# A feed-forward stage's weight sums, from VectorE to accumulating DMAs of GpSimd, with another order of products

## The reference

```
h = h + mixed @ w_out
u = relu(rms_norm(h, norm_ffn) @ w_up)      # 1024 -> 4096
y = h + (u * u) @ w_down                    # 4096 -> 1024
```

## Time and profile before

| | |
|---|---|
| median of 3 runs | 1353.36 us (1352.21 to 1353.92) |
| profiled execution, device time | 1355.98 us |
| its span, first to last instruction | 1353.9 us |
| mean granted TensorE clock | 0.997 |

### The profile page before, as it was taken

The page is one execution under the profiler, slowest core; times in us unless marked ns, Lnnn a source line. Parts: engine busy times, 40 slices in busy tenths (PEclk is TensorE's granted clock), DMA queues, the critical chain, the costliest instruction groups (busy, mean ns, idle before and its releaser), DMA issues.

```text
span 1353.9 us, 31255 instructions
## 1 busy us (share of the span) xinstructions
PE 1330.7 (98%) x10947; PEld 1267.4 (94%) x10947; DVE 880.7 (65%) x1805; ACT 658.6 (49%) x1617; POOL 277.5 (20%) x469
## 2 busy tenths in 40 slices
PE   7999999999999999999999999999999999999998
PEld 7877888999999999999989998899999999999998
DVE  5775665446657566475564666555569978868688
ACT  5653333366656556566553555532234444344442
POOL 0510000255545555455510000000230000000000
PEclk9999999999999999999999999999999999999999
DMA  6033221466555555665544645334341332423412
GB/s 248 20 100 108 80 84 57 146 178 186 160 150 167 173 160 160 174 183 153 164 154 163 208 147 192 121 103 125 106 157 50 102 133 63 141 63 95 140 46 97
DMA packets 110645, 177.92 MB, mean 131 GB/s; under 512 B 13217, under 2 KB 84706, under 8 KB 108770
## 3 DMA queue, kind: packets, MB, share of 16 engines
q1 hardware_dynamic: 110498, 176.05, 42.2%
HBM read 163.98 MB, written 11.89 MB: 130 GB/s over the span
## 4 chain that ended last, share of the span: by engine, by line
PE 86%; DVE 3%; issue 1%; ACT 1%; POOL 0%; ACTq 0%; DVEq 0%; POOLq 0%
PE ps L1382 27%; PE ps L2617 14%; PE ps L2640 10%; PE ps L1844 10%; PE ps L1669 8%; PE ps L659 5%; PE ps L1408 2%; PE ps L725 1%; PE ps L745 1%; PE ps L1398 1%; PE ps L1895 1%; PE ps L1884 1%; PE ps L735 1%; PE ps L1898 1%; PE ps L1390 0%
## 5 line engine op out<-in xcount | busy, mean ns | idle before, releaser
L1382 PE MATMUL ps<-wq_hi,ct_hi 128*128 128x260 f32 x1024 | 301.4, 294 | 1.4 <-POOL ct_lo L1064 1.4
L1382 PE MATMUL ps<-wq_hi,ct_lo 128*128 128x260 f32 x1024 | 289.5, 283 | 0.0
L1382 PE MATMUL ps<-wq_lo,ct_hi 128*128 128x260 f32 x1024 | 289.3, 283 | 0.0
L1229 DVE TENSOR_REDUCE k_sums<-k_squares 128x8 f32<-128x512 f32 (+1 forms) x256 | 175.2, 684 | 174.3 <-ACT k_squares L1127 171.9
L1064 POOL TENSOR_TENSOR ct_lo<-ct_raw,ct_hi 128x256 fp32r<-128x256 f32 x256 | 188.8, 738 | 359.6 <-ACT ct_hi L1120 197.1
L1127 ACT ACTIVATE k_squares<-ps 128x512 f32<-128x512 f32 x256 | 153.2, 598 | 169.5 <-PE ps L1382 165.3
L1382 PEld LDWEIGHTS ps<-wq_hi,ct_hi 128*128 128x128 f32 x1024 | 193.1, 189 | 4.9 <-issue 3.8
L1382 PEld LDWEIGHTS ps<-wq_lo,ct_hi 128*128 128x128 f32 x1024 | 193.2, 189 | 0.0
L1382 PEld LDWEIGHTS ps<-wq_hi,ct_lo 128*128 128x128 f32 x1024 | 192.6, 188 | 0.0
L1844 PE MATMUL ps<-x_hi,ring_hi 128*128 128x260 f32 x384 | 113.2, 295 | 1.4 <-DVE gates L2073 1.4
L1844 PE MATMUL ps<-x_lo,ring_hi 128*128 128x260 f32 x384 | 108.5, 283 | 0.0
(11 more groups left out here) (369 smaller groups left out, 3452.7 us busy)
## 6 DMA issues: line engine op xcount, KB each, us to landing
ct_raw<-in_ct SPq DMA_DIRECT2D x256, 144.0 KB, 2.3
c_values<-in_c SPq DMA_DIRECT2D x256, 128.0 KB, 2.4
ring_raw<-in_wmain SPq DMA_DIRECT2D x40, 512.0 KB, 4.2
ring_raw<-in_up SPq DMA_DIRECT2D x16, 512.0 KB, 3.5
ff_raw<-in_up SPq DMA_DIRECT2D x16, 512.0 KB, 4.6
ring_raw<-in_down SPq DMA_DIRECT2D x16, 512.0 KB, 3.5
ff_raw<-in_down SPq DMA_DIRECT2D x16, 512.0 KB, 3.5
z_scratch<-z_staged SPq DMA_DIRECT2D x16, 268.0 KB, 4.5
```

The costliest lines, as they stand in the source:

```text
L1229: dve.tensor_reduce(to, k2[:, j].rearrange("p b h d -> p (b h) d"), AX.X, ALU.add).then_inc(red_done, 1)
L1382: mm = nc.tensor.matmul(k_ps[j % 2][:, f, 0:WQN], ch[:, j, r * P:(r + 1) * P], of_sequence(w, b)[:, r, f, :], start=(r == 0 and x == 0), s ...
```

## The change

The four sums of a step are no longer made by VectorE. ScalarE writes -a0, -a1 and -a0 into the buffers of P6, P3 and P7 (`negate`). SP loads b0 from memory a second time, straight into P5's buffer. GpSimd then issues four DMAs that add to what is there: b1 onto P5's buffer (from memory), P5's sum onto P6's, P6's sum onto P3's, and b0 onto P7's (from memory). Of tile b only the second half is still loaded into the raw buffer. P3's and P7's sums now have the opposite sign, and so have B22 and T3. The weights of w_down are laid out on the host so that a half is contiguous.

The order of a step is P1, P5, P6, P3, P7, P2, P4, step after step with no interleaving. ScalarE's upper parts run two events behind and VectorE's lower parts three. The blocks of u are made one by one in the order in which the products use them, and the last of those of the final two up tiles are made in the down stage, after the additions of P1 and P5 of step 0.

```diff
     def gpsimd(self, pool):
         self.after.gpsimd(pool)
+        self.last.gpsimd(pool)
...
-P1, P2, P6, P5, P7, P3, P4 = range(UNITS)
+P1, P5, P6, P3, P7, P2, P4 = range(UNITS)
-ORDER = [(0, P1), (1, P1), (0, P2), (1, P2)] + [(d, x) for d in range(2) for x in (P6, P5, P7, P3, P4)] + [(d, x) for d in (2, 3) for x in range(UNITS)]
+ORDER = [(d, x) for d in range(STEPS_DOWN) for x in range(UNITS)]
+PLACE = {P2: (0, 0), P3: (0, 1), P4: (1, 0), P7: (1, 1)}
+SCALED = [(d, x) for d, x in ORDER if x in PLACE]
...
-ADDS_AHEAD = 4
+HI_BEHIND, LO_BEHIND = 2, 3
...
-BEHIND = _behind()
+HI_AFTER, LO_AFTER = _behind(HI_BEHIND), _behind(LO_BEHIND)
+NEGATED = {2: [(0, P6), (0, P3), (0, P7)], 6: [(1, P6)], 8: [(1, P3)], 9: [(1, P7)]}
+NEGATED.update({AT[d - 2, P4] + n: [(d, x)] for d in (2, 3) for n, x in enumerate((P6, P3, P7))})
...
-        a, b = (self.raw[n][:].rearrange("p (k two) n -> p two k n", two=2) for n in (2 * d % 4, 2 * d % 4 + 1))
+        a, b = (self.raw[n][:].rearrange("p (two k) n -> p two k n", two=2) for n in (2 * d % 4, 2 * d % 4 + 1))
...
+    def down(self, c, t, half):
+
+        return self.m.d_down[c // 2][c % 2][t][:, 4 * half:4 * half + 4, :]
+
+    def sum_ready(self, engine, n, x):
+
+        if x == P7:
+            engine.wait_ge(self.diff_sum, 16 * n + 16)
+        else:
+            engine.wait_ge(self.chain_sums, 48 * n + {P5: 16, P6: 32, P3: 48}[x])
+
+    def sum_split(self, engine, n, x):
+
+        c, d = divmod(n, STEPS_DOWN)
+        self.split(engine, PER_CHUNK * c + AT[d, x])
...
-                    d = (n0 - UP_TILES) // 2
-                    self.split(sp, PER_CHUNK * c0 + AT[d, P4 if n0 % 2 else P2])
-                    sp.wait_ge(self.summed, self.sums_at(c0, d, P7 if n0 % 2 else P3))
-            src = m.d_up[UP_TILES * c + n] if n < UP_TILES else m.d_down[c // 2][c % 2][n - UP_TILES]
-            sp.dma_start(self.raw[r % 4][:], src).then_inc(self.loaded[r % 4], 16)
+                    d0 = (n0 - UP_TILES) // 2
+                    self.split(sp, PER_CHUNK * c0 + AT[d0, P4 if n0 % 2 else P2])
+                    if n0 % 2 == 0:
+                        sp.wait_ge(self.negated, 3 * (STEPS_DOWN * c0 + d0) + 3)
+            raw = self.raw[r % 4]
+            if n < UP_TILES:
+                sp.dma_start(raw[:], m.d_up[UP_TILES * c + n]).then_inc(self.loaded[r % 4], 16)
+            elif n % 2 == 0:
+                sp.dma_start(raw[:], m.d_down[c // 2][c % 2][n - UP_TILES]).then_inc(self.loaded[r % 4], 16)
+            else:
+                sp.dma_start(raw[:, 4:8, :], self.down(c, n - UP_TILES, 1)).then_inc(self.loaded[r % 4], 16)
+                g = STEPS_DOWN * c + (n - UP_TILES) // 2
+                if g:
+                    self.sum_split(sp, g - 1, P5)
+                    self.sum_ready(sp, g - 1, P6)
+                sp.dma_start(self.sums[P5][:], self.down(c, n - UP_TILES, 0)).then_inc(self.plain_in, 16)
...
         elif x in self.sums:
-            act.wait_ge(self.summed, self.sums_at(c, d, x))
+            self.sum_ready(act, STEPS_DOWN * c + d, x)
...
+    def negate(self, act, c, d, x):
+
+        g, r = STEPS_DOWN * c + d, 16 * c + UP_TILES + 2 * d
+        act.wait_ge(self.loaded[r % 4], self.loads(r))
+        if g:
+            self.sum_split(act, g - 1, x)
+        if g and x == P6:
+            self.sum_ready(act, g - 1, P3)
+        half = 4 * (x == P3)
+        self.nc.scalar.activation(self.sums[x][:], self.raw[r % 4][:, half:half + 4, :], ACT.Copy, scale=-1.0).then_inc(self.negated, 1)
...
                 self.made(act, e)
-                wait(act, self.u_lo, 4 * (4 * c + i))
+                wait(act, self.u_lo, 7 * pair)
                 nc.scalar.activation(self.rl[s][:], ps[s][:, :, 0:HF], ACT.Relu).then_inc(self.relu, 1)
                 act.wait_ge(self.relu, UP_TILES * c + j + 1)
                 if s == 0:
-                    nc.scalar.activation(self.uh[:, B11, i, :], self.rl[0][:, 0, :], ACT.Square).then_inc(self.u_hi, 1)
+                    nc.scalar.activation(uh[:, B11, i, :], self.rl[0][:, 0, :], ACT.Square).then_inc(self.u_hi, 1)
+                    act.wait_ge(self.u_step, 6 * pair + 2)
+                    nc.scalar.activation(uh[:, T1, i, :], t[:, 0, :], ACT.Copy).then_inc(self.u_hi, 1)
                 else:
-                    nc.scalar.activation(self.uh[:, B21:B22 + 1, i, :], self.rl[1][:], ACT.Square).then_inc(self.u_hi, 1)
-                    for n in range(2):
-                        act.wait_ge(self.u_step, 6 * (4 * c + i) + 4 + 2 * n)
-                        nc.scalar.activation(self.uh[:, T1 + 2 * n:T3 + 2 * n, i, :], self.t[:, 2 * n:2 * n + 2, :], ACT.Copy).then_inc(self.u_hi, 1)
-            for n in REFILLED[e]:
-                self.split_hi(act, n)
+                    nc.scalar.activation(uh[:, B21, i, :], self.rl[1][:, 0, :], ACT.Square).then_inc(self.u_hi, 1)
+                    act.wait_ge(self.u_step, 6 * pair + 4)
+                    nc.scalar.activation(uh[:, T2, i, :], t[:, 1, :], ACT.Copy).then_inc(self.u_hi, 1)
+                    nc.scalar.activation(uh[:, B22, i, :], self.sq[1][:, 1, :], ACT.Copy, scale=-1.0).then_inc(self.u_hi, 1)
+                    act.wait_ge(self.u_step, 6 * pair + 5)
+                    nc.scalar.activation(uh[:, T3, i, :], t[:, 2, :], ACT.Copy).then_inc(self.u_hi, 1)
+                    act.wait_ge(self.u_step, 6 * pair + 6)
+                    nc.scalar.activation(uh[:, T4, i, :], t[:, 3, :], ACT.Copy).then_inc(self.u_hi, 1)
+            for done in HI_AFTER[e]:
+                for n in REFILLED[done]:
+                    self.split_hi(act, n)
+            for d1, x1 in NEGATED.get(e % PER_CHUNK, ()):
+                self.negate(act, c, d1, x1)
...
+        def low(kind, i, of, at):
+
+            dve.wait_ge(self.u_hi, at)
+            tt(self.ul[:, kind, i, :], of, self.uh[:, kind, i, :].bitcast(F32), ALU.subtract).then_inc(self.u_lo, 1)
...
+            dve.wait_ge(self.relu, UP_TILES * c + 2 * i + 1)
+            wait(dve, self.u_step, 6 * pair)
+            wait(dve, self.u_lo, 7 * pair)
+            tt(self.sq[0][:], self.rl[0][:], self.rl[0][:], ALU.mult).then_inc(self.u_step, 1)
+            dve.wait_ge(self.u_step, 6 * pair + 1)
+            tt(t[:, 0, :], self.sq[0][:, 1, :], self.sq[0][:, 0, :], ALU.subtract).then_inc(self.u_step, 1)
+            low(B11, i, self.sq[0][:, 0, :], 7 * pair + 1)
+            dve.wait_ge(self.u_step, 6 * pair + 2)
+            low(T1, i, t[:, 0, :], 7 * pair + 2)
+
+        def take_second(c, i):
+            pair = 4 * c + i
+            dve.wait_ge(self.relu, UP_TILES * c + 2 * i + 2)
             tt(self.sq[1][:], self.rl[1][:], self.rl[1][:], ALU.mult).then_inc(self.u_step, 1)
             dve.wait_ge(self.u_step, 6 * pair + 3)
-            dve.wait_ge(self.u_hi, 4 * pair + 2)
-            tt(self.ul[:, B21:B22 + 1, i, :], self.sq[1][:], self.uh[:, B21:B22 + 1, i, :].bitcast(F32), ALU.subtract).then_inc(self.u_lo, 1)
             tt(t[:, 1, :], self.sq[1][:, 1, :], t[:, 0, :], ALU.subtract).then_inc(self.u_step, 1)
-            tt(t[:, 2, :], self.sq[1][:, 1, :], self.sq[0][:, 1, :], ALU.subtract).then_inc(self.u_step, 1)
+            tt(t[:, 2, :], self.sq[0][:, 1, :], self.sq[1][:, 1, :], ALU.subtract).then_inc(self.u_step, 1)
             dve.wait_ge(self.u_step, 6 * pair + 4)
+            low(T2, i, t[:, 1, :], 7 * pair + 4)
+
+        def take_third(c, i):
+            pair = 4 * c + i
+            dve.wait_ge(self.u_hi, 7 * pair + 5)
+            nc.vector.scalar_tensor_tensor(self.ul[:, B22, i, :], self.sq[1][:, 1, :], -1.0, self.uh[:, B22, i, :].bitcast(F32),
+                                           ALU.mult, ALU.subtract).then_inc(self.u_lo, 1)
+            dve.wait_ge(self.u_step, 6 * pair + 5)
             tt(t[:, 3, :], self.sq[1][:, 0, :], t[:, 1, :], ALU.subtract).then_inc(self.u_step, 1)
-            for h in range(2):
-                dve.wait_ge(self.u_hi, 4 * pair + 3 + h)
-                tt(self.ul[:, T1 + 2 * h:T3 + 2 * h, i, :], t[:, 2 * h:2 * h + 2, :], self.uh[:, T1 + 2 * h:T3 + 2 * h, i, :].bitcast(F32),
-                   ALU.subtract).then_inc(self.u_lo, 1)
+            low(T3, i, t[:, 2, :], 7 * pair + 6)
+
+        def take_last(c, i):
+            pair = 4 * c + i
+            low(B21, i, self.sq[1][:, 0, :], 7 * pair + 3)
+            dve.wait_ge(self.u_step, 6 * pair + 6)
+            low(T4, i, t[:, 3, :], 7 * pair + 7)
...
-        def block_sum(c, d, x):
...
-            tt(self.sums[x][:], one, two, op).then_inc(self.summed, 1)
...
             else:
                 add(c, d, x)
-            for done in BEHIND[e]:
+                if (d, x) == (0, P1):
+                    take_third(c, UP_TILES // 2 - 1)
+                if (d, x) == (0, P5):
+                    take_last(c, UP_TILES // 2 - 1)
+            for done in LO_AFTER[e]:
                 c0, j0, d0, x0 = place(done)
-                if c0 == CHUNKS - 1 and x0 in (P2, P7, P3, P4):
```

(58 more changed lines are left out.)

38 lines of the change are left out of this document (14 added, 24 removed).

## The result

The changed kernel takes 1410.83 us (median; 1409.01 to 1413.73), the kernel before 1353.64 beside it (1352.21 to 1354.24): ratio 1.0422, 95% interval 1.0404 to 1.0439, some 57 us slower. The forecast was 1368.5 with a range up to 1400: the sign was right, the size far too small.

A forecast was written before the change was run, and what follows sets the result against it. TensorE bounds the kernel, with 2.43 us of VectorE waits in the fourth down stage. Terms -2.4 + 1.6 + 16.0 = +15.2 us on 1355.98 gave 1371.2, or 1368.5 as median; eight-in-ten range 1351.5 to 1400.

The forecast's parts named there:

- the timetable: Down stage, from its first matmul: second load at 8.05 us, 1.85 from P7's landing to P6, stalls in steps 2 and 3.
- -2.4 + 1.6 = -0.8: Fourth down stage loses its VectorE waits (-2.4 us); each down stage's first P6 waits 0.4 (+1.6); chain excluded.
- Part 4: Down stages: three chained accumulations per step outlast TensorE's 10.13 us, costing +4.0 us per chunk, +16.0 in all.
- A: Time of one 256 KB accumulating transfer from issue to landing, taken as 4.0 us; the chain hides up to 3.38.
- the plain half: SP's second load, 256 KB into P5's buffer before step 2's accumulations, taken to land in 2.7 us.
- that pushes up, not down: Remark that accumulations share the DMA engines with 1 MB of loads per step; no time was added for it.
- 4 x (40.53 + 0.4 + 4.0): Four down stages, each 40.53 us of matmuls, 0.4 wait at the first P6 and 4.0 of chain stalls.
- with 12 us to spare: Next chunk's up loads, queued on SP behind the late transfers, would still come in time; no cost.
- Steps 0 and 1 are covered: Down stage: sums of the first two steps begin in the up stage, so no wait for them there.
- rival (b): Accumulations crowd with loads, A is 4.5 or more, clock falls in stalls: 1394 us at 4.5, 1426 at 5.8; chance 0.21.
- 13.8 us for the clock: Part of rival (b): eight stalls, each costing 1.7 us of matmuls at a lowered clock.
- ScalarE's negations lie below that: Step 2 of a down stage: negations (first at 12.6 us) come before the accumulations need them; no cost.

The follow-up runs named there:

- e8: Changed kernel with all four accumulations cut to a quarter of the bytes (64 KB) and none waiting for another's sum: 1353.25 us, ratio 0.9986 to the kernel before.
- e5: Changed kernel with 6, 30 and 40 unused matmuls ahead of P6 of steps 1 to 3, keeping TensorE busy: 1408.60 us.
- e2: Changed kernel with P3's accumulation taken off the chain, adding half of b from memory in place of P6's sum: 1382.36 us.
- e11: Changed kernel with P5's sum made by VectorE from b loaded whole, without the second load and P5's accumulation: 1391.20 us.
- e12: e11 with the negations for steps 2 and 3 two events earlier in ScalarE's order: 1371.40 us.
- e10: Changed kernel with SP's weight loads moving a quarter of their bytes from the ninth load on, chain and accumulations whole: 1392.17 us.
- e15: e10 with the negations for steps 2 and 3 two events earlier in ScalarE's order: 1388.81 us.
- e13: Changed kernel with only the negations for steps 2 and 3 moved two events earlier in ScalarE's order: 1406.99 us.

## Why the prediction was wrong

- **Right: what bounds, and the small terms.** The changed kernel's path leaves TensorE for the chain of accumulations, at P6, behind the addition of P1, and P7's landing ends it. The first P6 of each down stage waits 0.38 us, four times (0.4 forecast). With the transfers made small (e8) the rest is -1.9 us (0.9986 of 1355), its interval from -3.4 to -0.3, where -2.4 + 1.6 = -0.8 stood.
- **Right: the timetable around the transfers.** Counted from the first down matmul (1051.45) the second load began at 7.9 us (8.05 forecast), and from P7's landing to P6 it took 1.9 (1.85).
- **Wrong: the size of the transfers in Part 4.** The mechanism was right; the step that failed is the one that took A at 4.0 and the plain half at 2.7, the latter from a row where it stood alone, and let "that pushes up, not down" count for nothing. The plain half took 7.05 with its hand-over (1059.31 to 1066.36), the six accumulations and P7's 30.6 in place of 25.0. That makes P6 of step 3 start at 47.4 us in place of 37.65, 9.8 later; in the other three stages it is 7.8, 7.8 and 6.3 later, 31.6 in all. The four down stages sum to 218.0 us against 4 x (40.53 + 0.4 + 4.0) = 179.7 forecast, 38.3 more: these 31.6, the 5.6 of slower matmuls behind them, which the sum put at nothing, and a wait of 0.9 for VectorE at the next product of the fourth stage. With the 2.7 us ahead of the change this is 41.0, about the miss of the profiled execution (1411.94 against 1371.2). TensorE waited 3.7 to 6.1 us at P6 of step 2 and 1.0 to 3.0 at that of step 3, where 2.1 and 1.9 stood. The next chunk's up loads, of which the prediction asked only whether they would be late ("with 12 us to spare"), are those beside which P6's accumulation of step 3 took 6 us.
- **Wrong: "Steps 0 and 1 are covered".** P7's accumulation of step 1 went out 6.8 us in, as forecast, and took 7.3 to land in place of 4.0, so P6 of step 1 waited 2.33 us (1.00, 1.30 and 0.85 in the later stages), where nothing stood. This isn't on the path, since the sums of step 2 came later still.
- **Alone, 4.0 was about right.** The shortest accumulations took 3.3 us from SBUF and 3.8 from memory, and the hand-over some 0.5: 3.8 to 4.3 a link. By the fit of the Trainium skill that the prediction weighed ("DMA: Bandwidth & Descriptors", section "Anatomy of one DMA — SWDGE (gpsimd) path", an estimate of 2.6 us) the chain would have been hidden; the measured 3.3 at the least decides against it.
- **Half right: rival (b).** Crowding did it, as (b) said from the same windows (0.34 busy before, twice the bytes to come). Of its 13.8 us for the clock less than half is in the time. The slower matmuls are real (TensorE was busy 46.7 us in the first stage where 40.53 would do), but most lie inside a stall; the 5.6 us behind the last stall of the first three stages are on the path, and e5, without any, is 2.2 us faster in the median. A price on the path and a price beside it were added.
- **Incomplete: one ring was counted.** The timetable follows P5, P6, P3, then the next P5. e2 and e11 show two more of 13 to 15 us: second load, P5, P6, second load (one buffer for P5's sum), and P6, P3, P7, ScalarE, negation, P6 ("ScalarE's negations lie below that"). Therefore shortening any one bought less than it should, and only e8, short in all, returns everything. e11 missed by such a ring, as the 20 us of e12 show. e2 and e10 missed by sizes once more: the ring of e2 was counted at 12.4 us and took 13.3 to 14.1, and in e10 the ring through ScalarE was worth 3 us (e15). In the changed kernel itself the ring through ScalarE costs little (e13).

## What to carry to other kernels

When work that an engine does in place becomes a chain of transfers, price each link at its landing under the load that it will itself bring, plus the hand-over, and compare every ring that closes through a single buffer or an engine's order with the time of one step. Experiments that shorten one ring are read only after asking which ring is next. A loss of clock inside a wait that another chain sets costs nothing by itself; slower matmuls behind the last wait do cost.
